# Regrouping four matmuls by the rows of their operands in the gate of a time-mixing layer

## The reference, cut to what matters

```python
g = jax.nn.sigmoid(xg @ g1) @ g2          # g1: 1024 x 160, g2: 160 x 1024
...                                       # w, k, v, a, the decay and the state
def step(state, inp):                     # over the tokens, for each of 16 heads
    r_t, d_t, k_t, v_t, kk_t, a_t = inp
    sa = jnp.einsum('bhij,bhj->bhi', state, -kk_t)
    state = (state * d_t[:, :, None, :] + sa[..., None] * (kk_t * a_t)[:, :, None, :]
             + v_t[..., None] * k_t[:, :, None, :])
    return state, jnp.einsum('bhij,bhj->bhi', state, r_t)
...
return (y * g.astype(f32)).astype(h.dtype) @ w_o
```

## Time and profile before

| | |
|---|---|
| runs, median (lowest to highest) | 1945.6 us (1944.59 to 1946.36) |
| profiled execution, its own time | 1940.4 us |
| its span, first to last instruction | 1938.6 us |
| TensorE busy | 1835.1 us, 95% of the span |
| mean granted TensorE clock | 0.971 |
| VectorE, ScalarE, GpSimd busy | 539.3, 395.9, 57.4 us |

### The profile page before, as it was taken

How to read it: one execution, slowest core, us unless ns; L and a number is a source line. 1 busy time by engine, 2 the same in 40 slices (tenths; PEclk the granted TensorE clock), 3 DMA queues, 4 the chain that set the end, 5 groups by cost and what they waited for, 6 DMA issues and landing times.

```text
span 1938.6 us, 21529 instructions
## 1 busy us (share of the span) xinstructions
PE 1835.1 (95%) x8558; PEld 1338.6 (69%) x8558; DVE 539.3 (28%) x1258; ACT 395.9 (20%) x1014; POOL 57.4 (3%) x71
## 2 busy tenths in 40 slices
PE   7999989999999998999988999899998999999998
PEld 5767768775577776777766768577776767557774
DVE  1000034743200002000066847300002444524353
ACT  1000022532200002000046312300002253212521
POOL 0300000000000000000002220000000000000000
PEclk9999999999999999999998959999998999999999
DMA  6754554112434433454533310245448663548620
GB/s 221 241 167 150 138 126 132 65 66 89 129 130 165 160 130 130 161 165 130 167 93 109 118 41 2 87 136 168 130 155 127 88 109 88 79 76 117 100 87 22
DMA packets 194134, 232.21 MB, mean 120 GB/s; under 512 B 27029, under 2 KB 175961, under 8 KB 194057
## 3 DMA queue, kind: packets, MB, share of 16 engines
q1 hardware_dynamic: 191584, 224.97, 42.5%
q0 software_dynamic: 1840, 5.12, 0.9%
q10 hardware_dynamic: 632, 1.04, 0.1%
HBM read 230.07 MB, written 1.05 MB: 119 GB/s over the span
## 4 chain that ended last, share of the span: by engine, by line
PE 90%; DVE 5%; ACT 2%; issue 2%; ACTq 0%; DVEq 0%
PE ps L503 32%; PE ps L273 24%; PE ps L521 14%; PE ps L460 6%; PE ps L1566 1%; PE ps L1401 1%; PE ps L544 1%; PE ps L356 1%; PE ps L2085 1%; PE ps L2101 1%; PE ps L2089 1%; PE ps L2115 1%; PE ps L2120 1%; PE ps L1583 1%; DVE x L416 0%
## 5 line engine op out<-in xcount | busy, mean ns | idle before, releaser
L503 PE MATMUL ps<-hT,ring 128*128 128x256 f32 x2816 | 625.8, 381 | 4.7 <-issue 4.7
L503 PEld LDWEIGHTS ps<-hT,ring 128*128 128x128 f32 x2816 | 537.9, 191 | 112.9 <-issue 43.3
L273 PE MATMUL ps<-hT,ring 128*128 128x272 f32 (+2 forms) x1504 | 361.9, 394 | 3.7 <-issue 1.3
L273 PEld LDWEIGHTS ps<-hT,ring 128*128 128x128 f32 (+1 forms) x1504 | 279.4, 190 | 64.6 <-issue 8.4
L521 PE MATMUL ps<-ring,arena 128*128 128x512 f32 x640 | 287.7, 592 | 0.0
L575 DVE TENSOR_TENSOR arena<-arena,ps 128x256 f32<-128x256 f32 x88 | 37.1, 421 | 856.4 <-ACT arena L560 856.4
L560 ACT ACTIVATE arena<-ps 128x256 f32<-128x256 f32 x88 | 33.7, 383 | 851.7 <-PE ps L503 851.7
L521 PEld LDWEIGHTS ps<-ring,arena 128*128 128x128 f32 x640 | 121.6, 190 | 118.9 <-issue 114.8
L460 PE MATMUL ps<-ring,arena 128*128 128x512 f32 (+1 forms) x192 | 86.6, 606 | 4.3 <-DVE more L1191 3.5
L460 PEld LDWEIGHTS ps<-ring,arena 128*128 128x128 f32 (+1 forms) x192 | 32.8, 178 | 56.4 <-issue 51.2
L356 PE MATMUL ps<-cst,arena 128*128 128x128 f32 x128 | 27.2, 394 | 37.9 <-DVE arena L436 37.9
(11 more groups left out here) (387 smaller groups left out, 1601.5 us busy)
## 6 DMA issues: line engine op xcount, KB each, us to landing
ring<-in_ffn_w_gate SPq DMA_DIRECT2D x44, 1024.0 KB, 5.3
ring<-in_ffn_w_up SPq DMA_DIRECT2D x44, 1024.0 KB, 5.3
ring<-in_ffn_w_down SPq DMA_DIRECT2D x44, 1024.0 KB, 5.0
ring<-in_w_in SPq DMA_DIRECT2D x32, 1024.0 KB, 10.5
ring<-in_ab_w_in SPq DMA_DIRECT2D x12, 1024.0 KB, 5.4
ring<-in_w_out SPq DMA_DIRECT2D x8, 1024.0 KB, 4.9
ring<-in_ab_w_out SPq DMA_DIRECT2D x6, 1024.0 KB, 4.8
ring<-in_c_w_k SPq DMA_DIRECT2D x4, 1024.0 KB, 5.5
```

The lines of the kernel that those rows point to most:

```text
L273: last = nc.tensor.matmul(o, l, r, start=(i == 0), stop=(i == len(pairs) - 1))
L503: m = nc.tensor.matmul(ps[:, 4 + j % 2, 256 * w:256 * (w + 1)], slot8(s0 + 3 * q + w)[:, k, c * P:(c + 1) * P], hT[:, k, META:], start=(k ...
```

## The change

The two calls of `g2_product` for t = 1 are written out, and their four matmuls are issued in another order: first the 128-row matmul of h = 0 and of h = 1, each into its own bank, then the 32-row matmul of h = 0 and of h = 1. Each accumulates into the same bank as before, and the increment of `to_act` stays on the 32-row matmul. The wait for `job["v", 0]` stands once ahead of all instead of once in each product. Both banks are now taken (`turn_a`) before the first product is complete.

```diff
+            o2 = []
...
-            g2_product(1, 0)
-            g2_product(1, 1)
+            pe.wait_ge(act_out, job["v", 0])
+            for rows in range(2):
+                for h in range(2):
+                    if rows == 0:
+                        n = turn_a("g2", 1, h)
+                        o2.append(bank_a(n))
+                        nc.tensor.matmul(o2[h], sg1[:, P:2 * P], slot2(s)[:, 0, h * 512:(h + 1) * 512], start=True, stop=False)
+                    else:
+                        nc.tensor.matmul(o2[h], sg2[:, P:2 * P], slot2(s)[0:32, 1, h * 512:(h + 1) * 512], start=False, stop=True).then_inc(to_act, 1)
             pe.drain().then_inc(slot_used, 1)
```

## The result

The changed kernel takes 1967.65 us in the median of 19 runs, against 1946.32 us for the kernel before in as many: ratio 1.0103, with a 95% interval of 1.009 to 1.0116. It is slower by 21.3 us. (The ratio is that of the means, without one run of the kernel before that took 6624.35 us; the medians alone give 1.0110.) Eighteen of the nineteen runs lie between 1965.3 and 1968.9 us with a mean granted clock of 0.955 to 0.957; one took 1946.83 us at 0.967, which is what the kernel before usually has.

A forecast was written before the change was run, and what follows sets the result against it. TensorE, busy 95% of the span, was taken as the bound. Terms 20.2 + 1.2 + 0.9 - 0.6 = 21.7 us on the median 1945.6 gave 1967.3 us, own range 1962.4 to 1971.5; for 8 in 10, 1943.9 to 1971.5.

The forecast's parts named there:

- The switches of size: Last two gate products: three switches between 128 and 32 rows become one, saving 2 x 0.29 = 0.59 us.
- D: Gate products: switch of size isn't what holds the loads back; no saving, no shift, 1945.6 us; chance 0.21 together with A.
- The rise missed: First chunk's opening: less dense work misses the clock's rise at 1161.76; next rise behind the second chunk's opening; chance 0.50.
- My count of the array's use: Work ahead of the rise: old stretch only little above stretches without a rise, shifted one about level with their best.
- The price: First chunk: 23.80 us of full-clock work at half clock, factor 1.85, costs 20.2 us, bounds 16.2 and 23.6.
- The opening of the second chunk: Its opening 24 matmuls at half clock take 2.93 instead of 1.74 us, costing 1.2 us.
- The later idle stretch: Idle stretch at 1247.10, about 21 us later: where work resumes relative to the next rise costs 0.9, bounds 0 to 1.7 us.
- A: First chunk: clock rises as before, only the two switches count, 1945.0 us; chance 0.21 together with D.
- B: Gate products: four back-to-back 128-row MATMULs bring the rise early, near 1153.2; 4.2 us saved, 1941.4 us; chance 0.21.
- C: First chunk: rise missed, but one of its passes brings it; 1953.5 us, down to 1950; chance 0.08.

The follow-up runs named there:

- padding experiment: Changed kernel with an extra 32-row matmul of 176 columns, result unread, behind the four, adding back 0.59 us: 1946.3 us, ratio 1.0003.
- the shortened one: Kernel before, old order, last 32-row matmul of product (1, 1) on 336 of 512 columns, products ending 0.59 us earlier: 1964.32 us, ratio 1.0089.
- exchanged order: Changed kernel with sizes exchanged: for t = 1 the two 32-row matmuls first, the two 128-row ones behind them: 1962.36 us, ratio 1.0082.
- 448 columns: Kernel before with the last 32-row matmul of product (1, 1) on 448 of 512 columns, 0.21 us earlier: 1952.59 us, ratio 1.0023.

## Why the prediction was right

**The switches of size.** 8.01 to 7.42 us in the chain, 0.59 us, as worked out; the padding experiment agrees from the other side, since 0.59 us of padding put the chunk's start back: from the first product's matmul to the chunk it is 1163.39 - 1155.15 = 8.24 us there and 1157.91 - 1149.64 = 8.27 in the kernel before. D falls.

**The rise missed.** As forecast, and the padded kernel and the shortened one separate shift from order: the shift is the cause. The next rise came where it was expected, too, at 1216.88, which is 1209.6 on the clock of the trace before (less 7.3 us, see below), against about 1209. What the prediction adds, that the rise is missed because the work ahead of the moment is less dense, is supported by the exchanged order alone, where dense work put there brought the rise earlier; it isn't shown. My count of the array's use gave no number that a run could meet, and I gave the forecast only 0.50. The argument was weakest where it said how near the old rise was to being missed. It was nearer than I needed: about 0.2 us of shift does it in seven executions of ten.

**The price.** The first chunk from its third set of 12 to the opening of the second chunk: 1212.99 - 1168.54 = 44.45 us. In the chain before that is 1185.63 - 1161.89 = 23.74 us (the earlier trace rows and the first line below, of the same chain). Difference 20.7; forecast 20.2. The pass took 6.14 against 3.29 us, a factor of 1.87, where I took 1.85. The opening of the second chunk cost 0.7 us, not 1.2. It starts 1212.99 - 1185.63 = 27.36 us later than before, and the matmul of the earlier trace rows, at 1190.44 there, 28.08 us later (second line, of TensorE's matmuls in the changed kernel). The wait for VectorE ahead of it shrinks from 1.08 to 0.47 us and takes up the rest:

```profile
1185.63 0.92 PE ps L1583 x12
...
1218.52 0.49 PE L1602 MATMUL ps<-gains 128*128 128x128 f32 x2 [0.47 <-DVE arena L1892]
```

**The later idle stretch** was the term mis-sized most: I put 0.9 us on where work would resume after it. Work resumes 1278.55 - 1250.49 = 28.06 us later than before, where it was 28.08 at the start of the second chunk; first the kernel before, then the changed one:

```profile
1250.49 3.62 PE L356 MATMUL ps<-cst,arena 128*128 128x128 f32 x16 [4.48 <-DVE arena L436]
...
1278.55 3.50 PE L356 MATMUL ps<-cst,arena 128*128 128x128 f32 x16 [4.48 <-DVE arena L436]
```

At the end of the spans the distance is 27.9 us, so the term was nought, or 0.2 us the other way. From the products' start to the end the kernels take 1966.5 - 1156.82 = 809.7 and 1938.6 - 1149.57 = 789.0 us, 20.7 apart; the terms as measured are -0.6, 20.7, 0.7 and -0.2. I had summed 21.7. The medians differ by 21.3. That the forecast hit the median within 0.4 us is in part luck: the terms' errors of 0.5, -0.5 and -1.1 us partly cancel, and the medians lie 0.6 us further apart than the two traces do from the products on.

**Own time and median.** The spans differ by 27.9 us, not by 20.7. The other 7.2 us lie ahead of the products, which start at 1156.82 instead of 1149.57, and they aren't the change's. The changed kernel's trace has a low stretch early in the program that the trace before lacks; first the kernel before, then the changed one:

```profile
305.50:319.20 13.70, 12.91 (x176) 11.22 (x179) 3.38 (x10) 5.37 (x14) 0.00 (x0) 1.00 0.63 194
```

```profile
305.50:319.20 13.70, 13.17 (x148) 11.74 (x148) 1.35 (x5) 3.83 (x8) 0.00 (x0) 0.50 0.55 166
```

Nine of the twelve traces have this stretch, 13.65 us long; one has a shorter one, and only those of the kernel before and of the exchanged order have none. At 307 us the two executions are some 2 us apart, at 429 us 7 us. Of the kernel before no other trace was kept, but its untraced runs mostly had a clock of 0.967 or 0.968 where the traced one had 0.971. So this stretch is probably what put the traced execution 5.2 us under the median. Adding a difference to the median, not comparing spans, was what kept the forecast of 1967.3 us close.

**The rivals.** By its time and clock, one run of nineteen was A; no trace of it was kept. No run of the changed kernel was near B's 1941.4 us. The exchanged order shows that such an early rise exists and, in the one trace, that it isn't kept. C is in the trace with 448 columns, and by time and clock in two runs with 336. The Trainium skill, "TensorE: Matmul & The Clock Gate", Part 1, has the gate's window running free of the kernel, and I had let that weaken the forecast. The two traces say that it matters less than it seems: they are 7.25 us apart at the products, yet from the fall to the products it is 1149.57 - 1120.80 = 28.77 us in one and 1156.82 - 1128.13 = 28.69 in the other. My explanation, argued and not shown: each time the clock rises in mid-work, a later moment means a longer piece at half speed, which moves the work half as far in the same direction, so that a dozen rises bring every execution to nearly the same place.

The same page's advice, in the section "Why this matters for your kernels", is that TensorE kept busy without a break gets the full clock. Here it doesn't hold: 88.33 of 88.70 us busy at 0.50. Much of that work was 32- and 64-row matmuls and 128x64 ones, which follow each other in 0.26 us (1.04 us for four), close to the 0.23 us of one weight load; whether that is the reason no run shows.

## What to carry to other kernels

Read the granted clock by stretches before pricing an edit beside a low one: a saving of 0.6 us was right to the hundredth and cost 21 us, because it moved the work against the moment at which the clock would have risen. Don't tune the place of the rise; remove the fall, by putting real products into the waits that the trace names, one after another, because the fall moves on to the next thin piece until all are filled. Filling only the first wait made this kernel slower (ratio 1.0127); with all of them filled, in part by two overwritten matmuls, it was 0.9% faster. And when one small edit shows a large effect, pad it back: if adding the saved time restores the old time, it was the shift.

## What the runs showed of the hardware that I had not expected

The low state can last while TensorE is busy: in one kernel 122.8 us at half clock with TensorE busy for 120.9 of them. A wait of 1.08 us in the second chunk lets the clock fall in one kernel and not in another. And the time is not a smooth function of the work: with 0, 0.11, 0.21 and 0.59 us taken out of the same matmul the medians were 1946.8, 1946.7, 1952.6 and 1964.3 us.
